# A two-layer hybrid decoder trunk on one core: the first scale and shift in four blocks, all copies of x on VectorE, the rotary angles behind the first norm

## The reference

```
inv_freq = ROPE_THETA ** (-arange(0, 32, 2) / 32)
ang = positions[..., None] * inv_freq ; cos, sin = cos(ang), sin(ang)
c_act = silu(c)
for l in range(2):
    mod = c_act @ ada_w[l] + ada_b[l]                  # (1, 6*1024)
    sh1, sc1, g1, sh2, sc2, g2 = split(mod, 6)
    h = rmsnorm(x, norm1_g[l]) * (1.0 + sc1) + sh1     # x: (1, 1024, 1024)
    proj = h @ w_in[l]                                 # columns for three mixers
    y = concat(ssd(proj), mla(proj, cos, sin), swa(proj)) @ w_out[l]
    x = x + g1 * y
    h = rmsnorm(x, norm2_g[l]) * (1.0 + sc2) + sh2
    x = x + g2 * gated_conv_mlp(h)
return rmsnorm(x, final_norm_g)
```

## Time and profile before

| what | value |
|---|---|
| median of 3 runs | 2311.76 us (2309.21 to 2312.41) |
| the profiled execution: its own time, its span | 2311.51 us, 2309.8 us |
| TensorE, VectorE, ScalarE, GpSimd busy | 97%, 71%, 48%, 44% of the span |
| mean granted TensorE clock | 0.993 of full |
| chain that ended last | TensorE 84%, VectorE 9%, issue 2%, ScalarE 2%, DMA 1% |

### The profile page before, as it was taken

How to read it: one execution, slowest core, us unless ns; L and a number is a source line. 1 busy time by engine, 2 the same in 40 slices (tenths; PEclk the granted TensorE clock), 3 DMA queues, 4 the chain that set the end, 5 groups by cost and what they waited for, 6 DMA issues and landing times.

```text
span 2309.8 us, 31053 instructions
## 1 busy us (share of the span) xinstructions
PE 2251.9 (97%) x11417; PEld 1835.7 (79%) x11417; DVE 1628.5 (71%) x2091; ACT 1100.6 (48%) x1813; POOL 1023.5 (44%) x659
## 2 busy tenths in 40 slices
PE   6999999999999999999999999999989999999998
PEld 4787867887788888888878787788878888888887
DVE  6895468449766676778888744772796766667886
ACT  4355557434444444444543464772454444444455
POOL 3222379345877777300012124053389777760000
PEclk8999999999999999999999999999999999999999
DMA  9732243341333333477557232114322333347763
GB/s 356 269 119 72 62 124 115 112 148 51 109 122 98 108 106 100 166 279 252 149 215 246 56 80 62 38 66 149 105 78 91 114 92 117 96 129 267 254 204 114
DMA packets 273222, 317.14 MB, mean 137 GB/s; under 512 B 33485, under 2 KB 187904, under 8 KB 272303
## 3 DMA queue, kind: packets, MB, share of 16 engines
q1 hardware_dynamic: 271359, 312.37, 41.9%
q10 hardware_dynamic: 1072, 2.23, 0.5%
q0 software_dynamic: 640, 0.55, 0.1%
HBM read 248.37 MB, written 62.54 MB: 135 GB/s over the span
## 4 chain that ended last, share of the span: by engine, by line
PE 84%; DVE 9%; issue 2%; ACT 2%; DMA 1%; POOL 1%; SPq 0%; DVEq 0%; ACTq 0%; POOLq 0%
PE bank L1610 31%; PE bank L1625 17%; PE bank L1129 17%; PE bank L1189 6%; PE bank L1452 1%; PE bank L1375 1%; PE bank L1501 1%; DVE hLo L2286 1%; DVE xT L2280 1%; PE bank L1279 1%; DVE xT L2651 1%; DVE tLo L2720 1%; PE bank L1423 1%; PE bank L1257 1%; PE bank L1424 1%
## 5 line engine op out<-in xcount | busy, mean ns | idle before, releaser
L1049 POOL TENSOR_TENSOR wLo<-raw,wHi 128x1024 fp32r<-128x1024 f32 x66 | 163.3, 2475 | 407.4 <-ACT wHi L1051 407.4
L1803 POOL TENSOR_TENSOR prodLo<-comb,prodHi 128x512 fp32r<-128x512 f32 x160 | 235.9, 1480 | 125.6 <-ACT prodHi L1091 125.6
L1610 PE MATMUL bank<-tHi,prodHi 128*128 128x512 f32 x640 | 250.3, 391 | 4.8 <-DVE tLo L2720 4.1
L1610 PE MATMUL bank<-tLo,prodHi 128*128 128x512 f32 x640 | 249.7, 390 | 0.0
L1610 PE MATMUL bank<-tHi,prodLo 128*128 128x512 f32 x640 | 249.6, 390 | 0.0
L1625 PE MATMUL bank<-gateHi,downHi 128*128 128x512 f32 x616 | 240.3, 390 | 0.0
L1625 PE MATMUL bank<-gateHi,downLo 128*128 128x512 f32 x616 | 239.7, 389 | 0.0
L1625 PE MATMUL bank<-gateLo,downHi 128*128 128x512 f32 x616 | 239.7, 389 | 0.0
L1091 ACT ACTIVATE prodHi<-comb 128x512 fp32r<-128x512 f32 x160 | 100.5, 632 | 248.6 <-PE bank L1610 231.1
L2665 DVE SCALAR_TENSOR_TENSOR ub<-bank,ffp,ub 128x1023 f32<-128x1023 f32 x88 | 112.8, 1282 | 143.4 <-ACT ub L2094 141.8
L1610 PE MATMUL bank<-hHi,prodHi 128*128 128x512 f32 x480 | 187.7, 391 | 7.3 <-POOL prodLo L1803 4.7
(11 more groups left out here) (422 smaller groups left out, 5399.7 us busy)
## 6 DMA issues: line engine op xcount, KB each, us to landing
raw<-in_ffn_w_up_dram SPq DMA_DIRECT2D x88, 512.0 KB, 5.0
gateRaw<-gateOut SPq DMA_DIRECT2D x154, 256.0 KB, 4.3
adaE<-in_ada_w_dram SPq DMA_DIRECT2D x64, 512.0 KB, 6.9
gateOut<-gateSums SPq DMA_DIRECT2D x22, 1024.0 KB, 5.6
raw<-in_w_in_dram SPq DMA_DIRECT2D x34, 512.0 KB, 4.3
downRaw<-in_ffn_w_down_dram SPq DMA_DIRECT2D x66, 256.0 KB, 3.6
raw<-in_w_out_dram SPq DMA_DIRECT2D x28, 512.0 KB, 4.3
downCols<-in_ffn_w_down_dram SPq DMA_DIRECT2D x24, 512.0 KB, 3.7
```

The costliest lines, as they stand in the source:

```text
L1049: eng.tensor_tensor(lo[:], raw[slot][:], fview(hi[:]), ALU.subtract).then_inc(s["split_lo"], 1)
L1610: last = mm(o, w[idx][:, c0], moving(idx, kp, hi), start=kp == 0 and q_ == 0, stop=kp == 3 and q_ == 2)
L1803: pool.tensor_tensor(sLoW[idx][:], product_source(js, idx), fview(sHiW[idx][:]), ALU.subtract).then_inc(s["us_lo"], 1)
```

## The change

The modulation for the first norm is made in four blocks of 256 columns instead of two of 512. Each block has its own weights in SBUF (one load per block and half, 1 KB rows), its own quarter of a PSUM bank, its own rows, turn and columns. FIRST_ORDER goes by two column tiles at a time. All eight copies of x are VectorE's. The load of the positions stands behind the sixth tile of x. Only the cast of the positions and the first multiplication stay in the prologue, behind the copies; the other nine angle instructions are the new function `rope_angles`, behind `first_apply`. The sine moves on ScalarE behind tile 3, and the store of its result on SyncE to tile 7.

The diff, cut:

```
-FIRST_ORDER = [(hf, KT // 2 * b + j) for b in range(2) for hf in range(2) for j in range(KT // 2)]
+N_BLOCK, BLOCK_COLS = 4, D // 4
+FIRST_ORDER = [(hf, 2 * b + j) for b in range(N_BLOCK) for hf in range(2) for j in range(2)]
...
             for t in range(NB):
                 sp.dma_start(xin[t][:], x[0, t * P:(t + 1) * P, :]).then_inc(s[f"x_loaded{t // 2}"], 16)
+                if t == 5:
+                    sp.dma_start(posi[64:128, :], positions.to_broadcast([64, T])).then_inc(s["pos_loaded"], 16)
             load_mod(0)
             load_win(sp, w_in[0:1], 1, 1, s["next_loaded1"])
-            load_mod(1)
+            for b in range(1, N_BLOCK):
+                load_mod(b)
...
             transpose_params(pe, prow)
+            spread_rms(pe, "n1")
             pe.wait_ge(s["c_act"], 1)
-            for kh in range(2):
-                mod_rows(pe, 0, 1, kh)
-            spread_rms(pe, "n1")
-            mod_rows(pe, 0, 0, 0)
-            mod_cols(pe, 0, 1)
-            mod_rows(pe, 0, 0, 1)
-            mod_cols(pe, 0, 0)
+            for g in (1, 0):
+                mod_rows(pe, 0, g)
+                mod_cols(pe, 0, g)
...
+            for t in range(NB):
+                dve.wait_ge(s["x_transposed"], t + 1)
+                dve.tensor_copy(xT[:, :, t * P:(t + 1) * P], bank[t % 2][:].rearrange("p (k t) -> p k t", k=KT)).then_inc(s["x_copied"], 1)
             dve.wait_ge(s["small_loaded"], 32)
             dve.wait_ge(s["pos_loaded"], 16)
+            dve.tensor_copy(nt[0][lo, :], posi[lo, :]).then_inc(s["pos_read"], 1)
+            dve.wait_ge(s["pos_read"], 1)
             link(dve.tensor_scalar(ang[lo, :], nt[0][lo, :], ropec[lo, 0:1], None, ALU.mult))
...
+                for b in range(N_BLOCK):
+                    k, more = 2 * b, b + 1 < N_BLOCK
+                    if b:
+                        steps(0, (k,))
+                    else:
+                        pe.wait_ge(s["next_lo"], 1)
+                        steps(0, (0, 1), (0,))
+                    if more:
+                        mod_rows(pe, b + 1, 1)
+                    if b:
+                        steps(0, (k + 1,))
+                    else:
+                        pe.wait_ge(s["next_lo"], 2)
+                        steps(0, (0, 1), (1,))
+                    if more:
+                        mod_rows(pe, b + 1, 0)
+                        mod_cols(pe, b + 1, 1)
+                    steps(1, (k,))
+                    if more:
+                        mod_cols(pe, b + 1, 0)
+                    steps(1, (k + 1,))
...
+            def rope_angles():
...
+                lo, ang, k = slice(64, 128), cs, nt[0]
+                dve.wait_ge(s["n1_lo"], 2 * KT)
+                fold_in(dve.tensor_scalar(k[lo, :], ang[lo, :], 1.0 / two_pi, ropec[lo, 1:2], ALU.mult, ALU.add), 1)
+                fold_in(dve.tensor_scalar(k[lo, :], k[lo, :], 12582912.0, None, ALU.add), 2)
+                fold_in(dve.tensor_scalar(k[lo, :], k[lo, :], -12582912.0, None, ALU.add), 3)
+                for n, q in enumerate(parts):
+                    fold_in(dve.scalar_tensor_tensor(out=ang[lo, :], in0=k[lo, :], scalar=-q, in1=ang[lo, :],
+                                                     op0=ALU.mult, op1=ALU.add), 4 + n)
+                fold_in(dve.tensor_scalar(ang[lo, :], ang[lo, :], ropec[lo, 2:3], None, ALU.add), 8)
+                fold_in(dve.tensor_scalar(ang[lo, :], ang[lo, :], 3.1415925, -3.1415925, ALU.min, ALU.max), 9)
```

More of the change, by code:

```diff
@@ L520, in build, with mod_part, mod_rows @@
     s["pos_loaded"], s["params_loaded"], s["next_loaded0"] = own["first_pos"], own["first_params"], own["first_win0"]
-    def mod_rows(pe, b, g, kh):
-        pe.wait_ge(s[f"mod_loaded{4 * b + 2 * (1 - g) + kh}"], 16)
-        for k in range(4 * kh, 4 * kh + 4):
+    def mod_part(b, g):
+        return half(3, g)[:, BLOCK_COLS * (b % 2):BLOCK_COLS * (b % 2 + 1)]
+    def mod_rows(pe, b, g):
+        pe.wait_ge(s[f"mod_loaded{2 * b + 1 - g}"], 16)
+        if b >= 2:
+            pe.wait_ge(s["mod_first"], 2 * b - 2 - g)
+        for k in range(KT):
             j = k % 4
[L527 to L530, removed]
+            last = pe.matmul(mod_part(b, g)[32 * j:32 * j + 32, :], cact[:, k:k + 1].to_broadcast([P, 32]), adaw[b][g][:, k, :],
+                             start=k < 4, stop=k >= 4)
+        last.then_inc(s["ada_rows"], 1)
     def mod_cols(pe, b, g):
@@ L535, in mod_cols @@
         for r in range(4):
-            last = pe.matmul(half(3, g)[32 * r:32 * r + 32, 0:4], quad[:], foldR[:, g, 32 * r:HALF:P], start=True, stop=True)
+            last = pe.matmul(mod_part(b, g)[32 * r:32 * r + 32, 0:2], quad[:], foldR[:, g, 32 * r:BLOCK_COLS:P], start=True, stop=True)
         last.then_inc(s["ada_cols"], 1)
@@ L868, in _ @@
                     else:
-                        sp.wait_ge(s["x_copied_act"], NB // 2)
-                        sp.wait_ge(s["x_copied_dve"], NB // 2)
+                        sp.wait_ge(s["x_copied"], NB)
                     sp.dma_start(xtail, xT[:]).then_inc(s["tail_saved"], 16)
-                if kind == "win" and m == 5 and not layer:
+                if kind == "win" and m == 6:
+                    sp.wait_ge(s["n1_lo"], nth("n1_lo", n1_done(1, KT - 1)))
+                    sp.wait_ge(s["tail_saved"], nth("tail_saved", 16))
+                    load_early(1, range(KT), 1)
+                if kind == "win" and m == 7 and not layer:
                     sp.wait_ge(s["rope_sin"], 1)
@@ L1960, in _ @@
                         A(darate, darate, ACT.Exp).then_inc(s["dt_act"], 1)
+                    if m == 3 and not layer:
+                        act.wait_ge(s["angle"], 9)
+                        A(cs[64:128, :], cs[64:128, :], ACT.Sin, scale=ropec[64:128, 3:4]).then_inc(s["rope_sin"], 1)
                     if m == 2:
@@ L2321, in _ @@
                 first_apply()
+                rope_angles()
             def step_sum():
```

121 lines of the change are left out of this document (39 added, 82 removed).

## The result

| | before | with the change |
|---|---|---|
| median of 16 runs each, same chip | 2309.81 us (2304.62 to 2318.52) | 2320.54 us (2315.73 to 2324.14) |
| ratio, 95% interval | | 1.0042 (1.0032 to 1.0052) |
| the profiled execution: own time, span | 2311.51 us, 2309.8 us | 2324.14 us, 2322.4 us |
| mean granted TensorE clock | 0.993 | 0.991 |

The change makes the kernel slower by 0.42%, some 9.7 us (the medians lie 10.7 apart). 2319.0 was forecast against 2320.54, and the range 2311.0 to 2322.5 holds it. Of all the executions behind this document one stands apart, of the kernel a_pos: 3879 us at a mean granted clock of 0.622, and it is left out of its ratio.

The account below looks back on a forecast made before the run. Up to 113.65 us TensorE and VectorE were both taken as the bound. A tap 5.2 us later plus 2.4 us of lost clock made +7.6 us, forecast as 2319 us, range 2311 to 2322.5.

Parts of the forecast that it names:

- What bounds: Up to the third convolution tap on tile 4 at 113.65 us, VectorE bounds as much as TensorE; neither has slack.
- Part 1: Start of the program: with all eight copies of x on VectorE, they end at 21.4 us, 3.0 us earlier.
- Part 2: First block's modulation: smaller rows and turns bring the first scaling to 29.4 us instead of 33.79, 4.4 us earlier.
- Part 3: Remaining norm blocks: TensorE and VectorE wait for each other, so the last low part ends at 68.0 us against 66.69.
- Part 4: VectorE's work from norm to tap, with the nine angle instructions: the tap ends at 118.8 us, not 113.65.
- The four hits: Behind the norm, four GpSimd weight splits each stretch VectorE's work by 2.1 us, 8.4 in all.
- Cover, stall and clock: TensorE reaches tile 6 at 113.8 us, stands 5 us for the tap, then loses 2.4 us at a lower clock.
- Sum: Whole kernel: +5.2 us for the later tap and +2.4 for clock make +7.6, giving 2319 us; chance 0.52.
- The full clock: Rival: TensorE keeps full clock in the first blocks, norm ends at 65.7; 2314.4 to 2316.8 us, chance 0.15.
- The second, GpSimd waiting instead: Rival: at splits GpSimd waits and VectorE doesn't, so TensorE's 113.8 decides; 2311 to 2313 us, chance 0.17.
- The third, a head start kept: Rival: VectorE isn't held at the turns, norm ends near 61.5, decisive before 63; time 2306 us, chance 0.08.
- The fourth, tile 7's load: Rival: longer waits between engines in the norm, or a late load for tile 7; 2322 to 2326 us, chance 0.08.

Follow-up runs that it names:

- a_pos: The changed kernel with the load of the positions issued ahead of x again, as before the change; 2320.47 us, ratio 1.0029 to the kernel before.
- b_behind: The kernel before with only the nine angle instructions moved behind the first norm, sine and angle stores later; 2318.79 us, ratio 1.0031.
- a_clamp: The changed kernel with only the last of the nine angle instructions left, the angles' range reduction left out; 2315.69 us, ratio 1.0014 to the kernel before.
- a_late: The changed kernel with the nine angle instructions moved behind the third and fifth pair of convolution tiles, sine and stores too; 2316.73 us, ratio 1.0027.
- a_rows: The changed kernel with both sets of the next block's modulation rows ahead of TensorE's projection steps in each block; 2313.50 us, ratio 1.0012.
- the second trace: A further profiled execution of the changed kernel, unaltered and timed again; 2321.74 us, ratio 1.0037 to the kernel before.
- a_two: The changed kernel with the first scale and shift in two blocks of 512 columns as before; 2316.73 us, ratio 1.0027 to the kernel before.
- a_shared: The changed kernel with the copies of x shared again between ScalarE (even tiles) and VectorE (odd); 2322.20 us, ratio 1.0045 to the kernel before.

## Why the prediction held, and where it didn't

**What bounds.** Right: before 113.65 us neither TensorE nor VectorE has anything to spare. b_behind shows it in one direction (only VectorE's list grows: TensorE stands 4.3 us), a_clamp and a_late in the other.

**Part 1, copies at 21.4.** Wrong in the change's own traces (24.53 and 23.55), first because I took the landing of 11.7 us from the earlier trace rows and wrote that the positions were "only placed elsewhere". Their place matters to the last tile: it took 13.5 and 12.9 us in those two traces, 1.8 and 1.2 more. The other 1 us or so is TensorE's clock, which this part doesn't count: the last sixteen transposes took 3.67 and 3.28 us, and 1.97 in a_pos. There, with the load put back, the copies ended at 21.10.

**Part 2, first scaling 8.0 us behind the copies, at 29.4.** Right in size: 8.5 in the profiled execution, 7.3 in a_rows. With part 1's miss the first scaling came at 33.06, in the second trace at 31.10.

**Part 3, the mutual waits.** The mechanism was right, and most of its numbers: second turn until +12 (+11.9), next block at +13.8 (+13.3), 9.1 us a block (9.1). Missed is the split of tile 2's weights: it fell on the gain of the fourth block, 2.37 us for 0.16. Without it the norm would have taken 37.6, 1 us under the forecast; with it, it took 39.9 instead of 38.6. Behind it I gave TensorE 2.2 us to tile 2, and it took 4.1: it had stood for 2.70 us and worked at a clock of 0.58 afterwards. In a_late, behind the same wait, the clock was 1.00 and the same way took 2.7, so 1.4 of the 1.9 missed here are clock.

**Part 4, the list.** Right: 50.8 us from the norm's end to the tap's end, 51.0 measured, and 50.9 in b_behind, a_two, a_shared, a_rows, a_pos and the second trace. The four hits came as forecast, and the idle time was filled. The tap ended at 123.94 instead of 118.8 because the norm ended 4.9 us later than forecast.

**Cover, stall and clock.** TensorE was to arrive at 113.8 and stand for 5; it arrived at 120.85 (3.7 from the start, 1.25 from the norm, 1.9 behind it, 0.2 in the tiles) and stood for 3.2. The clock then cost 1.6, not 2.4. Of the 10.3 us by which tile 6 is late, the end of the norm has 6.2 (72.91 for 66.69) and the list behind it 4.1; I had given them 1.3 and 3.9. So the list was right and the norm's end was the term that was too small. It delays both engines, and with VectorE's list out of the way TensorE is still late: undoing only the order of its rows gives back more (5.8 to 7 us) than moving the nine away (2.3 to 3.5).

**Sum.** 5.2+2.4 = 7.6 was forecast; 10.3+1.6 = 11.9 is in the profiled trace, 10.5 in the second, 9.7 by the ratio of the times. The miss of 4.3 in the first is 5.1 of later tile 6, less 0.8 of clock. That 2319 lies only 1.5 us from 2320.54 is in part luck: the median of the kernel before over sixteen executions is 2309.81, 2 us below the 2311.76 I started from, and the loss itself was forecast 2 to 3 us too small.

**Rivals.** The full clock fell: 0.50 stands in the window of the first block (38.60 to 42.10), 0.58 and 0.57 in those further on. The second, GpSimd waiting instead, fell too: between 64 and 124 us VectorE lost 2.1 to 2.2 us five times out of five. Read with the Trainium skill (SBUF — State Buffer, "Who interferes with whom"), whoever issues first has the shared ports for a whole instruction and the other blocks. The rows fit that, but not evenly: the splits at 89.45 and 111.21 met a running instruction of 1.3 us near its end and took 2.72 and 2.63 instead of 2.40, so GpSimd seems to have waited 0.2 to 0.3 us for it, and VectorE's next instruction took 3.3, 2 us more. In the trace before, a split that met such an instruction near its start (at 74.17) took 3.36. By these rows the long one loses at most the rest of one short instruction. The third, a head start kept, is what a_rows shows to be possible in this order of work: its norm ended at 63.07, just above the 63 under which I said it would decide, and the list was then the bound. The fourth, tile 7's load, wasn't seen: no wait for that tile's weights.

## What to carry to other kernels

When two engines are both without slack at the same point, cost each one's arrival there, not just the later one's: here TensorE was 7 us late and VectorE 10, 6 of them from the same late norm, and undoing either cause alone gave back only part. Cutting a stage into smaller blocks multiplies the places where two engines wait for each other; before it is cut, put what the other engine needs for its next block ahead of the work that waits for that engine's current one, which was worth 5.8 to 7 us here. And work moved off one busy stretch must be checked against the busy share of the stretch it goes to: nine instructions of 1 us each cost 5.6 us (by the trace) to 7.2 (by the times) behind the norm, and 0.7 to 1.6 us, which can't be told from nothing, spread over the convolution and scan.

## What the runs showed of the hardware

- An instruction of VectorE on two columns waited for a GpSimd split as long as one on 1024: 2.37 us for 0.16, against 2.85 for 0.69 and 2.32 for 0.22. The last two read one SBUF tensor, so such instructions are hit as well. The three taps, which read PSUM and SBUF, took 3.91 us together, as many as in the trace before, though a split ran from 122.08 on beside the second and third. A hit can be smaller where the split is already under way: at 36.20 a low part of 0.75 took 2.34, beside a split that began at 35.61.
- The same wait of TensorE, 2.7 us in the same place, stands in six traces. It was followed over 3.9 us by a clock of 0.58, 0.70 and 0.69 in three (the change twice, a_pos) and of 1.00 in the other three (a_clamp, a_shared, a_late), and tile 2 came 4.1 to 4.2 us behind the norm in the first, 2.7 in the others. Nothing in the rows tells why; it was not tried. The window in a_late, against 69.20:73.10 above:

```profile
67.49:71.40 3.91, 3.91 (x16) 2.95 (x17) 3.74 (x6) 1.45 (x2) 0.00 (x0) 1.00 0.45 139
```

- A load of 0.25 MB between the tiles of x moved the landing of the last tile by about 1.1 us on the mean (11.5 to 12.6), and made it spread by 2.5 us instead of 0.5 over nine traces and five.
